# Sample attention over a paged cache, rewritten with four sequences in column tiles and pages read by the sync queue

## The reference

```python
# layer 0, "NSA", 8 heads of 64 over 2 key heads
kc, vc = compress(k_cmp, w_cmp_k), compress(v_cmp, w_cmp_v)  # 32 tokens -> 1
p_c = masked_softmax(q @ kc);  o_c = p_c @ vc
top = top_k(sum_of_heads(p_c), 16)           # blocks of 64 tokens
o_s = softmax(q @ k_sel[top]) @ v_sel[top]
o_w = softmax(q @ k_win) @ v_win             # last 512 tokens
o = g0 * o_c + g1 * o_s + g2 * o_w
# layer 1: "diff" (4 heads, two softmax maps of 64, values of 128)
#          "DSA" (8 heads of 64, the 256 tokens with the highest index score)
o_diff = rmsnorm((p0 - lam * p1) @ v);  o_dsa = softmax(q @ k[top]) @ v[top]
```

## Time and profile before

| | us |
|---|---|
| median of 3 runs | 2696.6 |
| the profiled execution: its own time | 2694.48 |
| its span, first to last instruction | 2692.7 |
| TensorE busy in the span | 2229.8 |
| VectorE busy | 1178.0 |
| ScalarE busy | 555.9 |
| GpSimd busy | 317.8 |

### The profile page before, as it was taken

One profiled execution on the slowest core, in us unless ns is written; L12 is line 12 of the kernel. 1 busy time (PEld: TensorE's weight loads), 2 busy tenths in 40 slices (PEclk: granted clock), 3 DMA queues, 4 the chain that ended last, 5 costly groups with the idle time before them and its releaser, 6 DMA issues. The chain is left out here.

```text
span 2692.7 us, 26611 instructions
## 1 busy us (share of the span) xinstructions
PE 2229.8 (83%) x10297; PEld 1473.9 (55%) x10297; DVE 1178.0 (44%) x2644; ACT 555.9 (21%) x1192; POOL 317.8 (12%) x392
## 2 busy tenths in 40 slices
PE   6599998879988887778999788677676799799796
PEld 2476664344445775656765455454232566478574
DVE  0211003777655232532249994574699211211343
ACT  0300011555530110011110000452333121111001
POOL 0010000044334100000100000112221111010000
PEclk9799998989999685888999998898789578856698
DMA  6311101400024422301111000002000434132121
GB/s 239 147 61 41 38 27 37 158 1 1 1 78 188 172 79 94 127 34 53 57 39 50 18 33 17 0 1 63 0 1 1 172 125 165 56 152 81 40 88 65
DMA packets 38442, 188.37 MB, mean 70 GB/s; under 512 B 8268, under 2 KB 8365, under 8 KB 21739
## 3 DMA queue, kind: packets, MB, share of 16 engines
q0 software_dynamic: 15760, 98.49, 9.8%
q1 hardware_dynamic: 22556, 88.18, 9.0%
HBM read 171.69 MB, written 19.12 MB: 71 GB/s over the span
## 5 line engine op out<-in xcount | busy, mean ns | idle before, releaser
L655 PE MATMUL banks<-hT,w_in 128*128 128x352 f32 x1632 | 491.5, 462 | 39.8 <-DVE qdT L721 18.8
L655 PEld LDWEIGHTS banks<-hT,w_in 128*128 128x128 f32 x1632 | 309.7, 191 | 218.8 <-DVE qdT L721 21.1
L2475 PE MATMUL banks<-w_out_parts,mix_parts 128*128 128x512 f32 (+1 forms) x864 | 205.2, 401 | 35.8 <-DVE w_out_parts L172 35.8
L651 PE MATMUL banks<-w_in,hT 128*128 128x264 f32 (+5 forms) x1008 | 222.1, 376 | 14.0 <-DMA w_in<-in_w_in 14.0
L2475 PEld LDWEIGHTS banks<-w_out_parts,mix_parts 128*128 128x128 f32 (+1 forms) x864 | 160.0, 186 | 83.4 <-DVE w_out_parts L172 40.1
L651 PEld LDWEIGHTS banks<-w_in,hT 128*128 128x128 f32 (+1 forms) x1008 | 173.9, 187 | 50.7 <-DMA w_in<-in_w_in 14.2
L1236 POOL TENSOR_SCALAR nsa_p<-nsa_p,nsa_sum,gates 128x640 f32<-128x640 f32 (+7 forms) x128 | 100.2, 794 | 223.9 <-DVE nsa_sum L1181 223.8
L763 ACT ACTIVATE mix<-banks 128x352 f32<-128x352 f32 x48 | 21.9, 464 | 411.7 <-PE banks L655 382.0
L1073 ACT ACTIVATE nsa_p<-nsa_p,nsa_negmax 128x640 f32<-128x640 f32 (+7 forms) x128 | 92.6, 725 | 27.7 <-DVE nsa_negmax L1062 27.3
L1062 DVE CUSTOM_DVE_ANT_0 nsa_p<-banks,wide_masks 128x640 f32<-128x640 f32 (+7 forms) x128 | 84.1, 703 | 23.0 <-PE banks L1048 23.0
L388 PE MATMUL banks<-ada_w,cT 128*9 128x256 f32 x384 | 89.0, 386 | 6.0 <-DMA ada_w<-in_ada 6.0
(11 more groups left out here) (524 smaller groups left out, 3387.0 us busy)
## 6 DMA issues: line engine op xcount, KB each, us to landing
w_in<-in_w_in SPq DMA_DIRECT2D x24, 1056.0 KB, 4.9
ada_w<-in_ada SPq DMA_DIRECT2D x24, 1024.0 KB, 4.8
w_out<-in_l_w_out SPq DMA_DIRECT2D x4, 2048.0 KB, 7.8
x_in<-in_x_prompt SPq DMA_DIRECT2D x1, 4096.0 KB, 14.9
sw_run<-in_state_l_win_kv SPq DMA_DIRECT2D x8, 512.0 KB, 7.3
x_after<-in_x_prompt SPq DMA_DIRECT2D x1, 4096.0 KB, 17.7
x_mid<-x_after SPq DMA_DIRECT2D x8, 512.0 KB
x_after<-x_mid SPq DMA_DIRECT2D x1, 4096.0 KB, 17.8
```

Of the source, the lines that this page charges most:

```text
L651: last = pe.matmul(bank[0:rows, 0:n], k.hT[:, a, r0:r0 + rows], w[:, j % slots, a, 0:n], start=(a == 0), stop=(a == KT - 1))
L655: last = pe.matmul(bank[:, 0:cn], w[:, j % slots, a, m * P:(m + 1) * P], k.hT[:, a, c0:c0 + cn], start=(a == 0), stop=(a == KT - 1))
L2475: last = pe.matmul(k.bank[u % 4][0:n, :], lhs, rhs, start=a == 0 and x == 0, stop=a == KT - 1 and x == 2)
```

## The change

- **Caches.** The host lays each page out as 64 rows of 2 KB (`key_rows`, `value_rows`): keys already turned, two key heads side by side, values in halves of 64 tokens. A page of the chosen-block cache or of DSA holds keys and values in 128 KB; for diff, keys and values are two such pages.
- **Loads.** `SampleRing` is a ring of 11 slots (layer 0) or 12 (layer 1) of 1 MB. A slot holds two pages of each of four sequences. SyncE fills it with eight transfers of 64 x 512; for each it loads the page's number from SBUF into a register. In layer 0 the first 11 slots are filled in the stage of the compressed attention, the rest in the next one.
- **Attention.** Four sequences make one unit, on 4 x 32 partitions of PSUM. The query rows are stationary (64 rows x 32 columns), 128 keys are moving, in eight places of the array: four columns, one a sequence, times two row halves, one a page. No keys are turned; the probabilities are, 128 x 128 at a time. The maximum is taken once a unit, over all its keys.
- **Compression.** It moves into `project` of layer 0: GpSimd gathers blocks of 32 tokens, one a partition, and VectorE multiplies and sums them (`reduce_blocks`, 16 times) between its unit copies.
- `diff_sample` and `dsa_sample` become one stage. The page numbers come in two transfers instead of eight.

The core of the diff:

```diff
+SAMPLE_DEPTH = (11, 12)
...
-                    for n in range(8):
-                        sp.dma_start(pages[16 * n:16 * n + 16, :], t["page_table"].rearrange("b (h n) -> n (b h)", h=2)[n].partition_broadcast(16)).then_inc(loaded, 16)
...
+                sp.dma_start(pages[:, :], t["pages"]).then_inc(loaded, 16)
+                sp.dma_start(k.page_list[:, :], t["page_list"]).then_inc(loaded, 16)
...
+        def gather_blocks(pool, n):
+
+            kv, s, half = runs[n]
+            pool.indirect_dma_start(cmp_run[:, n % 2, :], None, t["cmp_blocks"],
+                                    bass.IndirectOffsetOnAxis(ap=k.cmp_rows[:, 2 * kv + half, s:s + 1], axis=0)).then_inc(cmp_loaded[n % 2], 16)
...
+        def reduce_blocks(dve, n):
+
+            kv, s, half = runs[n]
+            dve.wait_ge(cmp_w_loaded, 16 * (kv + 1))
+            dve.wait_ge(cmp_loaded[n % 2], 16 * (n // 2 + 1))
+            v = cmp_run[:, n % 2, :].rearrange("p (j g d) -> p j g d", j=HC, g=2)
+            w = cmp_wr[:, half * HC * HD:(half + 1) * HC * HD].rearrange("p (j d) -> p j d", j=HC).unsqueeze(2).to_broadcast([P, HC, 2, HD])
+            k.dve_order.link(dve, dve.tensor_tensor(v, v, w, ALU.mult))
+            last = dve.tensor_reduce(cmp_half[:, :] if half else k.kvc[:, kv, s, :], cmp_run[:, n % 2, :].rearrange("p (j c) -> p c j", j=HC), X, ALU.add)
+            k.dve_order.link(dve, last)
+            dve.sem_inc(cmp_reduced, 1)
+            if half:
+                k.dve_order.link(dve, dve.tensor_tensor(k.kvc[:, kv, s, :], k.kvc[:, kv, s, :], cmp_half[:, :], ALU.add))
...
+                    load_weights(pool, 0)
+                    gather_blocks(pool, 0)
+                    gather_blocks(pool, 1)
...
+                    for n in range(2, len(runs)):
+                        pool.wait_ge(cmp_reduced, n - 1)
+                        if n == len(runs) // 2 + 1:
+                            load_weights(pool, 1)
+                        gather_blocks(pool, n)
...
+                    if i in cmp_after:
+                        reduce_blocks(dve, cmp_after[i])
...
+    def load(self, pool, first, last):
+
+        for n in range(first, min(last, len(self.chunks))):
+            u, kind, h, c = self.chunks[n]
+            un = self.units[u]
+            if n >= self.depth:
+                sem, count = self.release[n - self.depth]
+                pool.wait_ge(sem, count)
+            un["load"](pool, kind, un["group"], h * un["pairs"] + c, self.ring[:, n % self.depth], self.loaded[n % self.depth])
...
+def gather_pairs(k, caches):
+
+    def load(sp, kind, group, pair, dst, loaded):
+        cache = caches[kind]
+        n = cache.shape[0] // HD
+        for j in range(GB):
+            for x in range(2):
+                u = 2 * ((GB * group + j) * PAIRS + pair) + x
+                page = sp.value_load(k.page_list[0:1, u:u + 1], min_val=0, max_val=n - 1)
+                sp.dma_start(dst[x * HD:(x + 1) * HD, j, :], cache[bass.ds(page * HD, HD), :]).then_inc(loaded, 16)
     return load
...
+            for h in range(un["halves"]):
+                s = R.step_at[(u, h)]
+                if s >= 2:
+                    pe.wait_ge(maxed, 2 * (s - 1))
+                bank = [k.bank[2 * (s % 2) + x] for x in range(2)]
+                if un["mask"]:
+                    for x in range(2):
+                        pe.matmul(bank[x][:, 0:un["pairs"] * P], *un["mask"](g, h, x), start=True, stop=False, skip_group_check=True)
+                for c in range(un["pairs"]):
+                    run = R.wait(pe, u, "keys", h, c)
+                    for b in range(un["blocks"]):
+                        for j in range(GB):
+                            for x in range(2):
+                                d = slice(x * HD, (x + 1) * HD)
+                                last = pe.matmul(bank[x][rows_of(j), c * P:(c + 1) * P], un["q"][d, b, GB * g + j, :],
+                                                 run[d, j, b * P:(b + 1) * P], start=not un["mask"] and c == 0 and b == 0,
+                                                 stop=b == un["blocks"] - 1, skip_group_check=True)
+                last.then_inc(R.scored, 1)
+
+        def turn(u, h, e):
+            g = group_at[(u, h, e)]
+            pe.wait_ge(exped, exps_until[u] + h + 1)
...
+            for c in (2 * e, 2 * e + 1):
+                run = R.wait(pe, u, "values", h, c)
+                if c == 2 * e:
+                    pe.wait_ge(copied[g % 2], g // 2 + 1)
+                for t in range(2):
+                    i = 2 * (c - 2 * e) + t
+                    for j in range(GB):
+                        last = pe.matmul(total[rows_of(j), 0:w], pT[:, g % 2, i * P + 32 * j:i * P + 32 * (j + 1)],
+                                         run[:, j, un["v_at"] + t * w:un["v_at"] + (t + 1) * w], start=first and i == 0, stop=False,
+                                         skip_group_check=True)
+                last.then_inc(R.freed, 1)
...
+        for u, un in enumerate(units):
+            scores(u)
+            behind = None
+            for _, h, e in [x for x in groups if x[0] == u]:
+                turn(u, h, e)
+                if behind:
+                    values(*behind)
+                behind = (u, h, e)
+            pe.wait_ge(exped, exps_until[u + 1])
+            pe.transpose(small[0:NS, P:2 * P], p[:, PAST:PAST + NS], k.const("ident")).then_inc(new_turned, 1)
+            values(*behind)
+            pe.wait_ge(new_copied, u + 1)
+            for j in range(GB):
...
+                    last = dve.tensor_tensor_reduce(dst, tiled(k.bank[2 * (s % 2) + x][:, 0:n]), tiled(m), -1.0, 3e38, ALU.add, ALU.min,
+                                                    nm[:, u, 2 * h + x:2 * h + x + 1])
...
+        units = [dict(common, group=g, halves=2, pairs=4, transfers=2 * GB, load=gather_pairs(k, {"both": t["sel_pairs"]}), mask=block_mask,
+                      window=None, k_new=[k.kT["sel"][:, new]], v_new=k.v["sel"][0:NS, RT - 1, :], finish=finish(1)) for g in range(GROUPS)]
+        units += [dict(common, group=g, halves=1, pairs=2, transfers=1, load=window_pairs(k), mask=None,
+                       window=k.mask("win_past"), k_new=[k.kT["win"][:, new]], v_new=k.v["win"][0:NS, RT - 1, :], finish=finish(2))
...
+                ring.load(sp, ring.depth, len(ring.chunks))
...
+                ring.load(sp, 0, ring.depth)
...
+        units = [dict(apart=True, blocks=4, q=k.diff_q, q_new=k.diff_q_new, width=2 * P, v_at=0, new_mask=k.tailb[:, :], group=g, halves=2, pairs=4,
+                      transfers=2 * GB, load=gather_pairs(k, {"keys": t["diff_k_pairs"], "values": t["diff_v_pairs"]}), mask=None, window=None,
+                      k_new=[k.diff_k_new[:, x, :] for x in range(2)], v_new=k.diff_v_new[:, :], finish=finish(acc)) for g in range(GROUPS)]
+        units += [dict(apart=False, blocks=2, q=q, q_new=q_new, width=P, v_at=2 * P, new_mask=sel[:, PAST:PAST + NS], group=g, halves=2, pairs=4,
+                       transfers=2 * GB, load=gather_pairs(k, {"both": t["dsa_pairs"]}), mask=key_mask, window=None,
+                       k_new=[k.kT["dsa"][:, new]], v_new=k.v["dsa"][0:NS, RT - 1, :], finish=finish(acc_d)) for g in range(GROUPS)]
...
+                ring.load(sp, 0, len(ring.chunks))
```

More of the change, by code:

```diff
@@ L1980, in gather @@
-def gather(k, caches, slots):
-    def load(block, run, loaded, free):
-        @block.gpsimd
-        def _(pool):
-            for u in range(DB * HALVES):
-                for n, cache in enumerate(caches):
-                    if u >= slots[n]:
-                        gone = u - slots[n] + 1
-                        pool.wait_ge(free[n], gone if n < len(caches) - 1 else -(-gone // HALVES) * HALVES)
-                    pool.indirect_dma_start(run[n][:, u % slots[n]].rearrange("p i n -> p (i n)"), None, page_rows(cache),
-                                            bass.IndirectOffsetOnAxis(ap=k.rows[:, u:u + 1], axis=0)).then_inc(loaded[n][u % slots[n]], 16)
-    return load
@@ new lines, in gather_pairs, with window_pairs, load @@
+def gather_pairs(k, caches):
[7 more added lines that the diff above has]
+                sp.dma_start(dst[x * HD:(x + 1) * HD, j, :], cache[bass.ds(page * HD, HD), :]).then_inc(loaded, 16)
+    return load
+def window_pairs(k):
+    def load(pool, kind, group, pair, dst, loaded):
+        pool.dma_start(dst[:, :, :], k.t["win_pairs"][GB * group:GB * (group + 1), pair].rearrange("j p n -> p j n")).then_inc(loaded, 16)
+    return load
@@ L2012, in spread_queries, with head_queries @@
+def head_queries(k, dve, st_q, st_new, qT):
+    for g in range(2):
+        src = qT[g * HD:(g + 1) * HD, :, SEQ:R].rearrange("p a (b t) -> p b a t", t=DS)
+        rows = lambda a: a[:, :, 16 * g:16 * g + 16].rearrange("p b (a t) -> p b a t", t=DS)
+        dve.tensor_copy(rows(st_new[g * HD:(g + 1) * HD, 0]), src)
+        for x in range(2):
+            last = dve.tensor_copy(rows(st_q[x * HD:(x + 1) * HD, g]), src)
     return last
```

(15 more changed lines are left out.)

836 lines of the change are left out of this document (389 added, 447 removed).

## The result

The changed kernel takes 2720.1 us (median of 4 runs, 2715.4 to 2722.5) against 2697.0 us before (4 runs, 2694.2 to 2698.3; the three of the first table are among them): a ratio of 1.0085, 95% interval 1.0067 to 1.0102. The forecast was 2570 us, faster. The time lies inside the range, on the side of the rival *Dear register reads*.

A forecast was written before the change was run, and what follows sets the result against it. TensorE bounded both sample stages; after the change SyncE's page issue was to bound layer 1. The two stages sum to 472 T + 132 = 580 us against 700, with `setup` -126, from 2694.5 to 2570 us; range 2430 to 2740.

The forecast's parts named there:

- Dear register reads: Sample attention: load and register work cost over 0.74 us a page; at T = 1.32, 2746 us, slower; chance 0.27.
- The bound after the change: Layer 1's sample attention: SyncE, bringing 384 pages one by one, becomes the bound in place of TensorE; 392 us against 427.
- 384 T + 27: Layer 1's sample attention: 384 page times on SyncE plus about 27 us after the last page, 392 us.
- T: SyncE's time for one page, register load, register work and transfer: 0.95 us taken, between 0.48 and 1.42.
- the form: Both layers' sample attention together: 472 T + 132 = 580 us, against 700 before.
- The lower bound of T: SyncE's page transfers in sample attention: 0.48 us apiece if load and register work are free.
- Cheap register reads: Sample attention: at T = 0.65 layer 0 takes 162 us and layer 1 277, 2430 us in all; chance 0.17.
- Layer 0: 105 us and 88 pages: Layer 0's sample attention: 88 T for pages issued first, then 105 us with the other 40 pages beside it; 189 us.
- the forecast's form: Layer 0's sample attention: 88 T + 105 = 189 us, against 273 before.
- 133 us at full clock and 266 at half: Layer 1's sample attention: TensorE's work on scores, values and turned probabilities, one instruction's time taken for each matmul.
- Tiles don't overlap: TensorE in sample attention: each matmul takes two instructions' time; -27 us, 2669 us in all; chance 0.08.
- the rule that speaks against the values: Layer 1's value matmuls: weight loads overlap only in another row group, so diff's stay near 68.1 us, not 27 to 54.
- `project`: 0 expected: Layer 0's `project`: the compression moved there, 4.5 to 6.5 us a run, is hidden; 32 us at most if not.

The follow-up runs named there:

- the four kernels: The changed kernel and, against it, fixed addresses, number loaded but unused, and no range check: 2720.1, 2414.5, 2620.4 and 2568.1 us.

## Why the prediction was wrong

**The bound after the change: right.** SyncE bounds layer 1. TensorE's idle time before the ring's matmuls ends on `ds_ring`, the pages come evenly, the ring never makes SyncE wait. 384 T + 27 is within 7 us for four values of T.

**T: the failing step.** The prediction took 0.47 us for load and register work, "nearer to" a small VectorE operation than to a gather, and T = 0.95. Measured: 0.789 and 1.266. For the load of the number with its use the 0.47 was good: 0.498, and with T = 0.966 the kernel runs in 2568 us, the very forecast (by some luck: its two sample stages took 564 us for the 588 that the form gives at this T, against 9 more in `project`). The range check was not priced apart. It stood in the instruction listing as two of the "three register instructions", which are four in the trace, and costs 0.29 to 0.30 us a page, 152 us in all, over 512 pages. The forecast missed the result by 150 us, so that this is as much as all of it; the smaller errors below cancel. The rival *Dear register reads* described what happened, at T = 1.32 for 1.266. The floor of about 600 ns that the Trainium skill gives a register load (DMA: Bandwidth & Descriptors, Latency and other measured facts) is not borne out as a price of the load: 0.268 us shown, 0.315 in the pace.

**The lower bound of T: wrong.** 0.48 from the earlier trace rows was read from other transfers, of the page table and of 512 KB. Single pages of 64 rows are issued every 0.66 us from the first ten on, without any register work; pairs start at 0.49. *Cheap register reads* at T = 0.65 was therefore the floor of this form of transfer; at 0.665 the run gave 2414 us for the 2430 of that rival.

**Layer 0: 105 us and 88 pages, the wrong split.** The stage follows 128 T + 48, a fit. All 128 pages count, by the slope over the four kernels: the last 40 are not hidden beside TensorE's work, as the prediction had it. The errors offset each other near T = 1.4: at 1.266 the forecast's form is 6 us high, at 0.665 31.

**TensorE: overestimated.** 133 us at full clock and 266 at half were expected; it was busy 114.6 us at 0.52. A slot of DSA, 16 score matmuls of 128 columns, took 1.11 us at the lower clock, 0.069 each for the 0.213 expected: eight places of the array overlap more than the pairs of the earlier trace rows. *Tiles don't overlap* is out. By the rule that speaks against the values (the Trainium skill, TensorE: Matmul & The Clock Gate, The mechanism) diff's alone would have stayed near the 68.1 us of the earlier trace rows; the group above has 41.1 us for those of diff and DSA together, at the lower clock. The gain on TensorE was real and larger than forecast, but the pages bound the stage.

**`project`: 0 expected, +9.7.** VectorE's products and sums were hidden: 2.29 + 3.67 us a run, inside the 4.5 to 6.5 taken. What was missed stands on GpSimd's queue. "GpSimd's gathers for it have no other user" looked at who waits for the gathers, and not at what is queued behind them: the stores, for whose buffers VectorE waits. **`setup`: -6 expected, -6.1.**

Summed with the measured T, the prediction's own form gives 472 x 1.266 + 132 = 730 us against 700: +30, and +24 with `setup`, for the +28 between the two spans. That this is so close is partly luck: +9.7 in `project` and +7.7 in small stretches stand against formulas 13 us too high.

## What to carry to other kernels

A transfer at an address from a register is an instruction sequence on the issuing engine, and each part has its price: here 0.32 us for the load, 0.29 for the range check, 0.18 for forming the address and 0.48 for the issue, all in series, 512 times. Before moving a gather to such a queue, multiply the full pace by the number of transfers and set it against the work that it should hide behind; then drop the check where the numbers are known to be in range, and share the transfers between two queues. When work is put on a queue, look at what already stands behind it there, not only at who uses the new work.

## What the hardware showed that was not expected

- Register instructions cost more than their shown durations: 0.170 shown and 0.291 paid for the check, 0.080 and 0.183 for the address.
- Transfers of 128 rows of 2 KB were issued faster than those of 64 rows: at fixed addresses 0.49 us each at the start for pairs, 0.66 for single pages, and 389 GB/s for 196. Whether the price lies in the number of rows or in the half of the partitions that each fills was not tried.
- GpSimd's gathers of 128 rows of 2 KB stalled TensorE between its own matmuls. Its idle time in issue in layer 1, over all its groups, fell with their number: 152 us for 192 gathers, 104 for 144, 59 for 96, and 13.5 for plain transfers of the same size on the same queue. By what path a gather holds up TensorE's instructions stays open. The kernel before has 48 gathers of 1 MB in that stage, and none of TensorE's groups there has idle time in issue; two of them are in the earlier trace rows.
- TensorE's clock was granted at 0.52 in layer 1 where it was busy 23% of the time, and 0.70 where it was busy 88%. While TensorE waited for pages the lower level cost nothing; in the 21 us behind the last page, where the clock was granted at 0.74, what it cost was not measured.
